# Two groups of token tiles in place of three, and two modulation chunks at once in two column groups of TensorE

## What is computed

```python
mod = silu(c) @ w_ada + b_ada                      # 1024 x 6144, for 1 + 8 conditions
h = rmsnorm(x, g1) * (1 + scale1) + shift1
proj = h @ w_in                                    # 1024 x 7168: q, k, v, u, gv, gate_a, gate_b
out_b = stick_breaking_attention(q, k, v)          # 8 heads x 128, strictly causal
                                                   # sample tokens also see 256 cached positions each
out_a = gelu(u) * (w_spatial (causal) . layernorm(gelu(gv)) + b_spatial)
merged = sigmoid(gate_a) * (out_a @ w_branch_a) + sigmoid(gate_b) * (out_b @ w_branch_b)
x = x + gate1 * (merged @ w_out)
h = rmsnorm(x, g2) * (1 + scale2) + shift2
q = h @ w_query                                    # 8 heads x 2 halves x 128
# scores with 2 x 128 sub keys; top 16 of each half, top 16 of the 256 sums: 128 experts a token
act = gelu(h . expert_down[e]);  y = sum over e of softmax_gate * act * expert_up[e]
x = x + gate2 * y;  return rmsnorm(x, g_final), k, v, gv
```

## Time and profile before

| | us |
|---|---|
| median of 3 runs (2340.33 to 2343.09) | 2343.03 |
| the profiled execution's own time | 2341.77 |
| its span, from the first to the last instruction | 2340.0 |
| busy in it: PE, VectorE, ScalarE, GpSimd | 1712.1, 1630.5, 802.8, 814.7 |
| moved by DMA | 841.14 MB, mean 359 GB/s |
| chain that ended last | DMA 28%, PE 27%, VectorE 22%, ScalarE 8% |

### The profile page before, as it was taken

One profiled execution on the slowest core, in us unless ns is written; L12 is line 12 of the kernel. 1 busy time (PEld: TensorE's weight loads), 2 busy tenths in 40 slices (PEclk: granted clock), 3 DMA queues, 4 the chain that ended last, 5 costly groups with the idle time before them and its releaser, 6 DMA issues.

```text
span 2340.0 us, 22796 instructions
## 1 busy us (share of the span) xinstructions
PE 1712.1 (73%) x7010; PEld 1189.8 (51%) x7010; DVE 1630.5 (70%) x3454; ACT 802.8 (34%) x2085; POOL 814.7 (35%) x647
## 2 busy tenths in 40 slices
PE   6998957988889666878777763766460677777776
PEld 2747956845778555644475752765450222222111
DVE  1011168748898878877985968888989866766764
ACT  1121013386345123238413213452122334443332
POOL 0000024324343324434433423443345444444432
PEclk9999978978989787987655586888685899999989
DMA  7786879977989979997896998999999999999997
GB/s 232 277 259 228 299 305 422 421 299 286 410 343 421 393 283 422 418 421 272 345 417 261 412 365 328 375 420 369 363 412 354 390 420 420 421 415 416 378 387 300
DMA packets 129310, 841.14 MB, mean 359 GB/s; under 512 B 15487, under 2 KB 20863, under 8 KB 33882
## 3 DMA queue, kind: packets, MB, share of 16 engines
q0 software_dynamic: 86512, 615.29, 65.3%
q1 hardware_dynamic: 37348, 217.83, 24.8%
q10 hardware_dynamic: 5328, 6.56, 0.8%
HBM read 824.39 MB, written 15.22 MB: 359 GB/s over the span
## 4 chain that ended last, share of the span: by engine, by line
DMA 28%; PE 27%; DVE 22%; ACT 8%; issue 7%; DVEq 5%; ACTq 1%; POOL 1%; SPq 0%; POOLq 0%
DMA gather_ring<-in_experts,expert_numbers 27%; PE bank L749 10%; PE bank L740 8%; DVE gather_ring L1575 7%; DVE expert_sums L1588 7%; PE bank L763 4%; PE bank L1003 3%; ACT L1234 1%; ACT L1091 1%; POOL gather_ring L672 1%; ACT expert_coefs L1238 1%; ACTq L1088 1%; DVEq L1538 1%; DVEq L1551 1%; ACT expert_acts L1234 1%
## 5 line engine op out<-in xcount | busy, mean ns | idle before, releaser
L672 POOL DMA_INDIRECT gather_ring<-in_experts,expert_numbers x576 | 781.0, 1356 | 1486.1 <-DVE expert_sums L1588 810.8
L1588 DVE SCALAR_TENSOR_TENSOR expert_sums<-gather_ring,expert_coefs,expert_sums 128x1024 f32<-128x1024 f32 x378 | 483.3, 1279 | 98.1 <-ACT expert_coefs L1238 96.3
L1575 DVE CUSTOM_DVE_ANT_0 gather_ring<-gather_ring,h_kept 128x1024 f32<-128x1024 f32 x384 | 468.4, 1220 | 90.7 <-DMA gather_ring<-in_experts,expert_numbers 89.7
L1003 PE MATMUL bank<-gather_ring,expert_sums 128*128 128x512 f32 (+1 forms) x768 | 386.3, 641 | 187.6 <-ACT expert_sums L1252 187.3
L1234 ACT ACTIVATE expert_acts<-expert_dots 128x1 f32<-128x1 f32 x576 | 116.4, 202 | 1026.7 <-DVE expert_dots L1575 1023.5
L749 PE MATMUL bank<-hT,weight_chunks 128*128 128x128 f32 (+2 forms) x2304 | 419.7, 345 | 56.5 <-ACT sigmoids L1164 18.1
L749 PEld LDWEIGHTS bank<-hT,weight_chunks 128*128 128x128 f32 x2304 | 384.6, 204 | 87.2 <-ACT qT L1142 14.5
L1003 PEld LDWEIGHTS bank<-gather_ring,expert_sums 128*128 128x128 f32 (+1 forms) x768 | 127.3, 181 | 446.2 <-ACT expert_sums L1252 240.6
L1575 DVE CUSTOM_DVE_ANT_0 gather_ring<-gather_ring,u_and_gv 128x1024 f32<-128x1024 f32 x192 | 234.3, 1223 | 147.7 <-DMA gather_ring<-in_experts,expert_numbers 147.3
L740 PE MATMUL bank<-weight_chunks,hT 128*128 128x256 f32 (+1 forms) x960 | 229.2, 401 | 23.8 <-ACT u_and_gv L1147 10.6
L740 PEld LDWEIGHTS bank<-weight_chunks,hT 128*128 128x128 f32 (+1 forms) x960 | 181.2, 191 | 68.5 <-issue 29.3
(11 more groups left out here) (206 smaller groups left out, 1753.5 us busy)
## 6 DMA issues: line engine op xcount, KB each, us to landing
weight_chunks<-in_w_in SPq DMA_DIRECT2D x84, 1024.0 KB
weight_chunks<-in_w_ada SPq DMA_DIRECT2D x24, 1024.0 KB
weight_chunks<-in_w_query SPq DMA_DIRECT2D x24, 1024.0 KB
weight_chunks<-in_w_branch_a SPq DMA_DIRECT2D x12, 1024.0 KB
weight_chunks<-in_w_branch_b SPq DMA_DIRECT2D x12, 1024.0 KB
weight_chunks<-in_w_out SPq DMA_DIRECT2D x12, 1024.0 KB
gather_ring<-in_experts,expert_numbers POOLq DMA_INDIRECT x576
u_and_gv<-in_cache_k SPq DMA_DIRECT2D x16, 512.0 KB, 10.9
```

The costliest lines, as they stand in the source:

```text
L672: pool.indirect_dma_start(out=ring[:, item % RING, :], out_offset=None, in_=experts, in_offset=bass.IndirectOffsetOnAxis(ap=expert[:, seq( ...
L1003: mm = nc.tensor.matmul(bank[b + half][0:n, :], by[:, r % KEPT, :], up[:, half * 512:(half + 1) * 512], start=(k == 0), stop=(k == TOPK * ...
L1575: nc.vector.tensor_tensor_reduce(out=down, in0=down, in1=h2_of(t), scale=1.0, scalar=0.0, op0=ALU.mult, op1=ALU.add, accum_out=dots[:, c:c ...
L1588: nc.vector.scalar_tensor_tensor(out=a, in0=up, scalar=coef[:, c:c + 1], in1=a, op0=ALU.mult, op1=ALU.add).then_inc(s_vsum, 1)
```

## The change

- `GROUPS = [[0, 1], [2, 3, SAMPLE]]`: two fronts, of 256 and 320 tokens. 96 chunks are loaded for them in place of 144. The rows of tiles 0 and 1 are woven with the front of 2, 3 and `SAMPLE`; those of 2, 3 and `SAMPLE` run alone. `EARLY = [True]`, `ROW_US = [3.8]`.
- The modulation takes two chunks at once (`WIDE` = 512 columns): the matmuls of the one write to partitions 0 to 8 of a bank, those of the other to 32 to 40, in turns. There are two buffers of two chunks each, which lie in slots 3 to 6 of the gather ring. Five pairs come before the first norm and seven after v.
- The x tiles are normed in the gv buffer and added to in `v_tokens`; `x_rows` is gone. `hT`, `qT`, `u_and_gv` and `sigmoids` are wider. The sample's keys and values lie in the row tables, its attention logs in `u_and_gv`.
- ScalarE waits for two loads (the conditions) in place of five before the first activation.
- Three tiles share the later sums: their PSUM banks are used in turn, and the third tile's matmuls wait for the end of the first.

```diff
-FIRST_MODS = 8
-NADA = NMOD * D // WC
-LAST = 2
+WIDE = 2 * WC
+FIRST_MODS = 5
+NADA = NMOD * D // WIDE
+LAST = 1
-GROUPS = [[0], [1, 2], [3, SAMPLE]]
+GROUPS = [[0, 1], [2, 3, SAMPLE]]
-WOVEN = [0, 1, 2]
-LATER = [3, SAMPLE]
+WOVEN = [0, 1]
+LATER = [2, 3, SAMPLE]
-EARLY = [False, True]
-DIRECT = [True, True, False]
-ROW_US = [4.0, 3.0]
+EARLY = [True]
+DIRECT = [True, False]
+ROW_US = [3.8]
...
-        n = len(ts)
-        for phase, count, each in (("norm1", 2 * n, 2.0), ("q", 8, 3.9), ("k", 4 * n, 4.4), ("v", 4 * n, 3.9)):
+        n, wide = len(ts), 3.9 * max(1.0, columns_of(g) / 256)
+        for phase, count, each in (("norm1", 2 * n, 2.0), ("q", 8, wide), ("k", 4 * n, 4.4), ("v", 4 * n, 3.9)):
...
+        pairs = [flat[:, s * 2 * D:(s + 2) * 2 * D].rearrange("p (c k n) -> p c k n", c=2, k=KC) for s in (3, 5)]
...
+            def load_pair(p):
+                if p >= 2:
+                    f = pair_fill(p - 2)
+                    sp.wait_ge(s_full[f % 4], f // 4 + 1)
+                for c in range(2):
+                    sp.dma_start(pairs[p % 2][:, c], wv["ada"][2 * p + c]).then_inc(s_pair[p % 2], 16)
...
-            load_phase(0, "first", "ada", 0, range(WBUF, FIRST_MODS))
+            load_phase(0, "q", "in", 0, range(WBUF))
+            for p in range(2, FIRST_MODS + 2):
+                load_pair(p)
+            load_x(0, x_res, s_xr[0])
...
-                    load_phase(0, "rest", "ada", FIRST_MODS * WC, range(NADA - FIRST_MODS))
+                    for p in range(FIRST_MODS + 2, NADA):
+                        load_pair(p)
...
-            def modulation(n, f):
-                w = weight(n)
-                out = take(f)
+            def modulation(p):
+                pe.wait_ge(s_pair[p % 2], 32 * (p // 2 + 1))
+                f = pair_fill(p)
+                w, out = pairs[p % 2], take(f)
                 for k in range(KC):
-                    mm = nc.tensor.matmul(out[0:NG, 0:WC], cT[:, k, :], w[:, k, :], start=(k == 0), stop=(k == KC - 1))
+                    for c in range(2):
+                        mm = nc.tensor.matmul(out[32 * c:32 * c + NG, 0:WC], cT[:, k, :], w[:, c, k, :],
+                                              start=(k == 0), stop=(k == KC - 1))
                 mm.then_inc(s_full[f % 4], 1)
...
+                if LATER.index(t) >= 2:
+                    pe.wait_ge(s_ended, LATER.index(t) - 1)
...
-            act.wait_ge(s_cond, 16 * 5)
+            act.wait_ge(s_c, 16 * 2)
```

More of the change, by code:

```diff
@@ L105, in __init__ @@
         self.fill = self.turn = 0
[L106 removed]
+        self.fills["first", 0] = 0
+        self.fill += FIRST_MODS
         for g, ts in enumerate(GROUPS):
@@ L136, with pair_fill @@
 PLAN = Plan()
+def pair_fill(p):
+    return PLAN.fills["first", 0] + p if p < FIRST_MODS else PLAN.fills["rest", 0] + p - FIRST_MODS
 def fill_base(g, phase):
@@ L202 @@
 CLOCK = clock()
-STRETCH_AT = [CLOCK["query", g, 5] for g in range(3)]
+STRETCH_AT = [CLOCK["query", g, 5] for g in range(len(GROUPS))]
 NEVER = 1.0e9
@@ L402, in build @@
         s_wload = [sem(f"s_wload{i}") for i in range(WBUF)]
+        s_pair = [sem(f"s_pair{i}") for i in range(2)]
         s_full = [sem(f"s_full{i}") for i in range(4)]
@@ L775, in _ @@
             pe.wait_ge(s_tfree[1], 1)
-            for n in range(FIRST_MODS):
-                modulation(n, fill_base(0, "first") + n)
+            for p in range(FIRST_MODS):
+                modulation(p)
             pe.wait_ge(s_small, NSMALL)
@@ L826, in _ @@
                 if g == 0:
-                    for n in range(NADA - FIRST_MODS):
-                        modulation(chunk_base(0, "rest") + n, fill_base(0, "rest") + n)
+                    for p in range(FIRST_MODS, NADA):
+                        modulation(p)
                 turned(pe, turn_base(g, "gate"))
@@ L1403, in front @@
                 if g == 0:
-                    for n in range(NADA - FIRST_MODS):
-                        add_bias(fill_base(0, "rest") + n, (FIRST_MODS + n) * WC)
+                    for p in range(FIRST_MODS, NADA):
+                        add_bias(p)
                     scaled_gain(4, g2row)
```

186 lines of the change are left out of this document (104 added, 82 removed).

## The result

The changed kernel takes **2371.22 us** (median of 4 runs, 2369.89 to 2375.59) beside 2342.69 for the kernel before: a ratio of 1.0126, 95% interval 1.0113 to 1.0139. It is slower by 28.5 us. The forecast was 2386, its own range 2355 to 2415; so the direction is the forecast one, and the growth is two thirds of the 43 us that was forecast. The profiled execution took 2370.24 us with a span of 2368.5.

What follows compares the result with a forecast made beforehand. PE bounds the exposed front, no single engine the woven stretch, DMA engines the rows alone: 488 + 1046 + 850 = 2384 us of span, 2386 with 1.8 us added. Own range 2355 to 2415; 8 in 10, 2308 to 2434.

Steps and rivals of the forecast that it cites:

- The exposed front: Time before the first gather, now the front part of tiles 0 and 1: predicted 488 us, against 323.9 before.
- modulation's later part: Seven later chunk pairs in the exposed front: predicted 36 us, 20 less than before.
- 5 x 5.8: Five later modulation pairs, each bound by its 2.1 MB transfer at 421 GB/s plus latency: 5.8 us each.
- The woven stretch: 256 rows of tiles 0 and 1 woven with the front of tiles 2, 3 and sample: predicted 1046 us.
- the prediction's last sign: Woven attention: forecast wrong if ScalarE is less busy than 85 of 101 us, since the stage's 147 us then shrinks.
- 183.2 now: latency and 48 rows, now 40; 178: Pages stage of the woven stretch: latency and 40 rows in place of 48, 178 us against 183.2.
- Part 3: Rows of tiles 2, 3 and sample run alone at 2.58 us each: predicted 850 us, against 512.1 before.
- The three quantities: Whole kernel: exposed front's length, time per woven row, and number of rows that can have 2.58 us set the time.
- (1): Rival: VectorE alone binds the woven stretch, 970 us there and 2310 in all; chance 0.21.
- (2): Rival: modulation's column groups do not overlap, a pair costs PE 6.4 to 6.9 us; +20, 2406 in all; chance 0.12.
- (3): Rival: PE becomes the woven stretch's bound and loses clock; +50, 2436 us in all; chance 0.12.
- (4): Rival: the change gives what it takes, woven stretch 1003 us, 2343 in all; chance 0.07.

Runs made afterwards that it cites:

- Experiments 3 and 4: Changed kernel with the seven later modulation pairs behind q, k, v and attention: 2355.85 us; then behind q, k and v only: 2350.05 us.
- Experiment 6: Planned woven-row time 3.6 us in place of 3.8, on the changed kernel with later pairs behind q, k, v: 2357.66 us; on that with VectorE's thinned addition: 2344.28.
- experiment 4: Seven later modulation pairs behind q, k and v, last pair ahead of attention: kernel before with pairs 2326.58 us, changed kernel 2350.05 us.
- experiment 5: Changed kernel with, one at a time, VectorE's row addition on 128 columns, half the second group's weight loads, half its PE products: 2340.46, 2368.21, 2354.32 us.
- experiment 1: Changed kernel with both chunks of a modulation pair in one column group, one after the other: 2381.86 us.
- experiments 6 and 7: Experiment 6, and the kernel before with new modulation, its first woven group choosing experts before tile 0's last rows, 4.57 us planned per row: 2398.59 us.

## Why the prediction was right, and where it was not

**The exposed front: 501, not 488.** Its terms, in us, each against the growth that PE's rows show from the earlier trace rows to the fence above:

| term | predicted | measured |
|---|---|---|
| start of q (modulation's first part, first norm) | +6 | +6.3 |
| q | +11.4 | +14.0 |
| k and v | +28 | +28.5 |
| modulation's later part | -20 | -10.4 |
| attention | +31 | +28.6 |
| u, gv | +23 | +22.5 |
| layer norm, gates, merge | +57 | +59.8 |
| out, second norm | +21 | +20.2 |
| query to the first scores | +6.5 | +7.6 |

The step that failed is the pair's price, "5 x 5.8": the five took 7.6 us each, not 5.8. I had 2.1 MB at the full 421 GB/s plus 0.8 us of latency. From 151.2 to 197.4 the DMA engines were at 0.76 and moved 293 GB/s. A load starts when PE is through with the pair two before, so both the landing and PE's work, itself at a granted clock below full, lie inside the cycle. Two windows of one such cycle, PE waiting and then in the second half of its work (columns as above):

```profile
158.30:162.50 4.20, 0.01 (x2) 0.00 (x0) 0.83 (x2) 0.00 (x0) 0.00 (x0) 0.84 1.02 429
167.40:172.30 4.90, 4.86 (x42) 1.84 (x38) 0.83 (x2) 0.00 (x0) 0.00 (x0) 0.94 0.52 152
```

The DMA engines are full while PE waits and half idle while it works, which a bound by transfer alone leaves out. Experiments 3 and 4 show that this is where the time lay: with the pairs under q, k and v the first gather of the changed kernel comes at 479.6. Of these 21.5 us, 6.2 come from the earlier start of q and 15.2 from the later pairs. The other terms, which came from PE's price of a column or a piece, are within 3 us. Two of them hide something. The first is right as a sum only: the modulation's first part ended 4.2 us later, not 2, and the norm behind it took 2.1 more, not 4. For q I set 27.8, PE's time at full clock, against a 16.4 that was not (u, the same work, takes 15.0); q ran at a granted clock of 0.88 before and 0.92 after, and took 30.2.

**The woven stretch: 1023, not 1046.** By stages, predicted and measured: query's rest, norm and q 104, 105.5; k and v 94, 89.7; attention 147, 141.9; pages 178, 159.5; u and gv 80, 84.6; layer norm, gates and merge 197, 205.5; out and second norm 95, 88.2; query 84, 81.2; last rows 67, 67.0. From the windows of the changed kernel:

```profile
606.60:696.30 89.70, 88.57 (x410) 67.16 (x408) 75.83 (x141) 28.84 (x91) 43.16 (x28) 1.00 1.01 421
696.30:838.20 141.90, 117.40 (x388) 62.44 (x388) 100.22 (x191) 117.05 (x194) 57.26 (x37) 0.89 0.76 278
838.20:997.70 159.50, 140.31 (x576) 120.88 (x576) 117.39 (x218) 41.53 (x113) 62.60 (x46) 0.53 0.90 365
1082.30:1287.80 205.50, 151.75 (x561) 108.67 (x561) 183.50 (x384) 87.96 (x180) 82.19 (x54) 0.87 0.88 353
```

In attention ScalarE is busy 117 of 142 us, a share of 0.82 beside the 85 of 101, 0.84, of before. By the letter of the prediction's last sign that is the weak side, and the stage is indeed shorter than its 147, but by 5 us only. The step that was mis-sized is the pages, "183.2 now: latency and 48 rows, now 40; 178": 159.5, 18.5 less, four fifths of the whole error. The other eight stages are off by up to 8.5 either way and nearly cancel. PE in the kernel before, at the two places where the sample's attention goes through ScalarE:

```profile
1237.35 1.96 PE L912 MATMUL bank<-row_tables,minus_since_keys 64*64 64x512 f32 x2 [21.12 <-ACT row_tables L1134]
...
1331.58 8.63 PE L749 MATMUL bank<-hT,weight_chunks 128*128 128x192 f32 x42 [14.43 <-ACT qT L1142]
```

and in the changed one:

```profile
914.84 1.96 PE L961 MATMUL bank<-u_and_gv,minus_since_keys 64*64 64x512 f32 x2 [7.84 <-ACT u_and_gv L1186]
...
997.71 12.55 PE L794 MATMUL bank<-hT,weight_chunks 128*128 128x320 f32 x40 [0.67 <-ACT qT L1194]
```

PE does the same work in both (140.0 us of 183.2 and 140.3 of 159.5). In the kernel before ScalarE came to its first copy of the scores at 1228.3, 12 us after PE had ended them at 1216.2, because coefficients of rows stood ahead, waiting for VectorE. In the changed kernel it was there first and waited 5.1 us for PE. So these 27 us of PE's waits were no latency, as my sum had it, but an effect of where rows stand in ScalarE's stream. That cause is read from the two traces. Experiment 6 supports it for the second wait: with nothing changed but the order of the rows it went from 0.68 to 10.23 us. No run moves the rows of the kernel before.

**Rows alone: 844, not 850.** The window of the changed kernel with the dot of L1634 alone (length, VectorE busy (x records), PEclk, DMA share, GB/s; two records a row):

```profile
1650.00:1850.00 200.00, 95.99 (x157) 1.00 1.01 420
```

That is 2.55 us a row where I had 2.58, with the DMA engines full. Part 3 was right.

**The net.** The three quantities that the prediction set the time by are the right ones. That the sum is only 15 us off is in part luck, since 13 too little in the front and 23 too much in the woven stretch have nothing to do with one another. With the modulation made equal (experiment 4) the spans differ by 28.5 us: the front gives +174.6 (304.97 to 479.55), the woven stretches -481.6 (1507.5 to 1025.9), the rows alone +335.5 (509.8 to 845.3). The medians differ by 23.5.

**The rivals.** (1) VectorE alone binds, 970 us: refuted by experiment 5, where it has a quarter less work and the stretch is 3% shorter. What holds some stages is PE or the transfers. (2) Column groups do not overlap: refuted by the 3.54 us a pair and experiment 1. Its price was near: without them the later part is 51 us, where the rival had 48. Its signs would have misled: the first gather at 501 and the later part at 45.1 lie nearer to its 508 and 48 than to the forecast's 488 and 36, for a reason that is not the rival's. The Trainium skill, "TensorE: Matmul & The Clock Gate", Part 3, has matmuls in different column groups run together; the trace agrees. Its other half, that a weight load overlaps a running matmul only in another row group, would have given 6.4 us a pair by the prediction's estimate; the trace has 3.54, and the measurement decides. The kernel before already spoke against it: a token-major piece with weight loads of 190 ns and a modulation chunk with loads of 92 ns, 16 records each and all in the same rows, both take PE 3.47 us. (3) PE binds and loses clock: the woven clock was 0.82, a merge chunk was 8.61 us, at full clock, and half of PE's products gave 12 us. PE does hold single stages (experiment 5), but the loss of clock did not come. (4) 1003 us, gain equals loss: not reached, 20 us short.

What stays open: how far the woven stretch would shrink if two of its limits were eased at once, which no run tries, and what the waits across ScalarE's written order, which experiments 6 and 7 show, cost over the whole stretch.

## What to carry to other kernels

Where phases are woven with a long stream of small steps in a fixed order, an engine at 0.8 over the stretch need not be its bound. Read each stage by itself, and take work away to see, before counting on what a faster engine would give: the next limit can stand right behind. A wait on one engine that seems to be free time may only move to the engine whose stream is in order ahead of it. Count a double-buffered load as its full cycle, and put work between the loads rather than loads behind one another; and look what else stands on the queue of those loads.

## What the runs showed of the hardware

- Two column groups with the same rows and 9 stationary columns each run side by side in float32: 64 matmul records in 7.08 us, and 13.98 us in one column group (experiment 1).
- Where PE waited for transfers between short bursts, the granted clock was lower: 0.78 from 151.2 to 197.4 us in the changed kernel, so a pair took PE 4.65 to 6.05 us in place of 3.54. In one column group, with waits of 0.67 us, each pair kept 6.99.
- A load issue on SP that is 0.4 us alone took 9.4 and 5.0 us for the two broadcast tables that followed right behind the modulation's stores. The same two took 1.2 and 0.4 us in the kernel before, where 20 us lay between.
